# Masked maxima in one operation, scores issued ahead of the sums, and a quarter of the copies on VectorE, in a two-block network on one core

## The reference

```python
# sparse attention: 8 heads of 64, one key and value head, the selected keys of a row as mask
s = einsum(q, k_g) * 64 ** -0.5;  s = where(valid, s, -inf);  p = softmax(s);  o = p @ v_g
# latent attention: 8 heads, keys of 96, causal;  paired attention: 8 score maps in 4 pairs, causal
p = p[0] - lam * p[1]          # paired: mixed before the values
# memory attention: 4 heads of 128 against 256 memory tokens, no mask
```

```python
s = concat([einsum(q_row, k_win) + bias, einsum(q_row, k_c)]);  p = softmax(s)
o = p_loc @ v_win + p_ctx @ v_c
```

## Time and profile before

| | |
|---|---|
| median of 3 runs | 4144.8 us (4137.83 to 4156.16) |
| profiled execution, its own time | 4138.23 us |
| its span | 4136.4 us |
| mean granted TensorE clock | 0.973 of full |
| busy: TensorE, VectorE, ScalarE, GpSimd | 3854.7, 1670.0, 1430.4, 1414.1 us (93, 40, 35, 34%) |

### The profile page before, as it was taken

The page is one execution under the profiler, slowest core; times in us unless marked ns, Lnnn a source line. Parts: engine busy times, 40 slices in busy tenths (PEclk is TensorE's granted clock), DMA queues, the critical chain, the costliest instruction groups (busy, mean ns, idle before and its releaser), DMA issues. The chain is left out here.

```text
span 4136.4 us, 57230 instructions
## 1 busy us (share of the span) xinstructions
PE 3854.7 (93%) x23428; PEld 3229.0 (78%) x23428; DVE 1670.0 (40%) x3370; ACT 1430.4 (35%) x2322; POOL 1414.1 (34%) x525
## 2 busy tenths in 40 slices
PE   6998989999989899999989989999999888889999
PEld 5766878887876678788769967888888777867887
DVE  5845152322384524332261464311124676754111
ACT  3434242342234423333232364211122544433221
POOL 2211323343321132234322322223222567643342
PEclk8899999999999999999999999999999999999999
DMA  3221414434222142344412211112222111103332
GB/s 116 56 83 40 139 54 141 122 118 127 76 56 83 39 130 64 120 119 142 127 51 72 75 25 32 51 52 76 62 57 71 43 42 52 41 17 88 91 98 74
DMA packets 476080, 323.18 MB, mean 78 GB/s; under 512 B 31449, under 2 KB 472236, under 8 KB 475820
## 3 DMA queue, kind: packets, MB, share of 16 engines
q1 hardware_dynamic: 422112, 268.18, 22.5%
q10 hardware_dynamic: 53708, 51.33, 3.7%
HBM read 315.74 MB, written 2.16 MB: 77 GB/s over the span
## 5 line engine op out<-in xcount | busy, mean ns | idle before, releaser
L96 POOL TENSOR_TENSOR w_lo<-w_raw,w_hi 128x2048 fp32r<-128x2048 f32 (+6 forms) x329 | 1157.5, 3523 | 2417.8 <-ACT w_hi L228 2417.4
L228 ACT ACTIVATE w_hi<-w_raw 128x2048 fp32r<-128x2048 f32 (+3 forms) x278 | 471.9, 1698 | 1113.8 <-PE psum L264 1068.2
L262 PE MATMUL psum<-xF_hi,w_hi 128*128 128x512 f32 x1232 | 493.3, 400 | 15.7 <-ACT a_relud L1673 6.8
L264 PE MATMUL psum<-xF_hi,w_lo 128*128 128x512 f32 x1232 | 484.3, 393 | 0.0
L263 PE MATMUL psum<-xF_lo,w_hi 128*128 128x512 f32 x1232 | 480.7, 390 | 0.0
L262 PE MATMUL psum<-ffn_h_hi,w_hi 128*128 128x512 f32 (+1 forms) x1056 | 376.5, 357 | 2.2 <-issue 1.3
L264 PE MATMUL psum<-ffn_h_hi,w_lo 128*128 128x512 f32 (+1 forms) x1056 | 375.0, 355 | 0.0
L263 PE MATMUL psum<-ffn_h_lo,w_hi 128*128 128x512 f32 (+1 forms) x1056 | 373.7, 354 | 0.0
L262 PEld LDWEIGHTS psum<-xF_hi,w_hi 128*128 128x128 f32 x1232 | 232.6, 189 | 69.9 <-ACT a_relud L1673 8.4
L264 PEld LDWEIGHTS psum<-xF_hi,w_lo 128*128 128x128 f32 x1232 | 232.1, 188 | 53.8
L263 PEld LDWEIGHTS psum<-xF_lo,w_hi 128*128 128x128 f32 x1232 | 232.2, 189 | 48.7
(11 more groups left out here) (554 smaller groups left out, 8183.4 us busy)
## 6 DMA issues: line engine op xcount, KB each, us to landing
w_raw<-in_w_in_dram SPq DMA_DIRECT2D x56, 1024.0 KB, 5.2
ada_w<-in_ada_w_dram ACTq DMA_DIRECT2D x48, 1024.0 KB, 6.9
w_raw<-in_ffn_w_in_dram SPq DMA_DIRECT2D x88, 512.0 KB, 5.1
w_raw<-in_w_in_dram SPq DMA_DIRECT2D x78, 512.0 KB, 4.2
w_raw<-in_ffn_w_out_dram SPq DMA_DIRECT2D x32, 704.0 KB, 4.6
w_raw<-in_w_branch_dram SPq DMA_DIRECT2D x74, 256.0 KB, 4.6
w_raw<-in_hg_w_in_dram SPq DMA_DIRECT2D x32, 512.0 KB, 4.8
w_raw<-in_na_w_qkv_dram SPq DMA_DIRECT2D x12, 1024.0 KB, 5.1
```

The costliest lines, as they stand in the source:

```text
L96: return eng.tensor_tensor(pair.lo, src, pair.hi.bitcast(F32), ALU.subtract)
L228: act.activation(self.w(j).hi, self.raw_w(j), ACT.Copy).then_inc(*self.high_done.up(1))
L262: pe.matmul(out, left.hi, right.hi, start=first, stop=False)
L264: return pe.matmul(out, left.lo, right.hi, start=False, stop=last)
```

## The change

In the masked case the reduction's scale goes into `tensor_tensor_reduce`: it writes the negated scaled scores and reduces with a minimum, straight into `bias`; the exponential then has scale -1. Without a mask and with scale 1 (the context units of the neighbourhood stage), `tensor_reduce` negates. The `tensor_scalar` remains for the memory stage alone. Each unit now signals its own maximum. In `paired_attention` the same, and the tile `top` is gone.

TensorE's order in `attention` becomes scores(0), then for each s: turn(s-1), scores(s+1), sums(s-2). VectorE's: its copies of s-1, the maxima of s+1, the result of s-2, the inverse of s-1. ScalarE's: the copies of s-1, the exponentials of s+1, the raising of a part. In the neighbourhood stage units 3, 7, 11, ... 95 are in `dve_copies`.

```diff
                 C.enter(pe)
+                scores(0)
                 for s in range(NU // 2 + 2):
-                    if s < NU // 2:
-                        scores(s)
                     turn(s - 1)
+                    if s + 1 < NU // 2:
+                        scores(s + 1)
                     if features:
                         feature_sums(s - 2)
...
                     if mask is None:
-                        step(dve.tensor_reduce(column(top, u), scores_at(u)[:, 0:N], AX.X, ALU.max))
+                        if scale == 1.0:
+                            dve.tensor_reduce(column(bias, u), scores_at(u)[:, 0:N], AX.X, ALU.max, negate=True).then_inc(*max_found.up(1))
+                        else:
+                            step(dve.tensor_reduce(column(top, u), scores_at(u)[:, 0:N], AX.X, ALU.max))
+                            dve.tensor_scalar(column(bias, u), column(top, u), -scale, None, ALU.mult).then_inc(*max_found.up(1))
                     else:
...
-                        step(dve.tensor_tensor_reduce(dst, src, mask, 1.0, -3.0e38, ALU.add, ALU.max, column(top, u)))
-                    if not features:
-                        dve.tensor_scalar(column(bias, u), column(top, u), -scale, None, ALU.mult).then_inc(*max_found.up(1))
-                    elif u % 2:
-                        dve.tensor_scalar(columns(bias, u // 2), columns(top, u // 2), -scale, None, ALU.mult).then_inc(*max_found.up(2))
+                        dve.tensor_tensor_reduce(dst, src, mask, -scale, 3.0e38, ALU.add, ALU.min,
+                                                 column(bias, u)).then_inc(*max_found.up(1))
...
-                for s in range(NU // 2 + 2):
-                    for u in group(s):
+                for s in range(-1, NU // 2 + 2):
+                    for u in group(s - 1):
+                        if u in dve_copies:
+                            copy(u)
+                    for u in group(s + 1):
                         highest(u)
                     if features:
-                        for u in group(s - 1):
-                            if u in dve_copies:
-                                copy(u)
                         if s >= 2:
                             feature_result(s - 2)
...
-                for s in range(NU // 2 + 1):
-                    for u in group(s):
-                        N = width(u)
-                        act.wait_ge(*max_found.at(u + 1))
-                        if u >= 4:
-                            act.wait_ge(*turned.at(u - 3))
-                        src = scores_at(u)[:, 0:N] if units[u]["mask"] is None else probs[u % 4][:, 0:N]
-                        act.activation(probs[u % 4][:, 0:N], src, ACT.Exp, bias=column(bias, u), scale=scale,
-                                       accum_out=column(den, u)).then_inc(*exped.up(1))
+                for s in range(-1, NU // 2 + 1):
                     for u in group(s - 1):
...
+                    for u in group(s + 1):
+                        N = width(u)
+                        act.wait_ge(*max_found.at(u + 1))
+                        if u >= 4:
+                            act.wait_ge(*turned.at(u - 3))
+                        src, by = (scores_at(u)[:, 0:N], scale) if units[u]["mask"] is None else (probs[u % 4][:, 0:N], -1.0)
+                        act.activation(probs[u % 4][:, 0:N], src, ACT.Exp, bias=column(bias, u), scale=by,
+                                       accum_out=column(den, u)).then_inc(*exped.up(1))
...
-                    step(dve.tensor_tensor_reduce(probs[:, u % 6, 0:N], scores_at(u)[:, 0:N], units[u]["mask"], 1.0, -3.0e38,
-                                                  ALU.add, ALU.max, column(top, u)))
-                    dve.tensor_scalar(column(bias, u), column(top, u), -scale, None, ALU.mult).then_inc(*max_found.up(1))
+                    dve.tensor_tensor_reduce(probs[:, u % 6, 0:N], scores_at(u)[:, 0:N], units[u]["mask"], -scale, 3.0e38,
+                                             ALU.add, ALU.min, column(bias, u)).then_inc(*max_found.up(1))
...
-            dve_copies=())
+            dve_copies=range(3, NAH * TA, 4))
```

More of the change, by code:

```diff
@@ L952, in paired_attention @@
         probsT, probs = sb("probsT", [P, 2, 512]), sb("probs", [P, 6, 512])
-        top, bias, den, rec = (sb(n, [P, 8]) for n in ("top", "bias", "den", "rec"))
+        bias, den, rec = (sb(n, [P, 8]) for n in ("bias", "den", "rec"))
         share = sb("share", [P, 4])
@@ L1079, in _ @@
                             N = width(u)
-                            act.activation(probs[:, u % 6, 0:N], probs[:, u % 6, 0:N], ACT.Exp, bias=column(bias, u), scale=scale,
+                            act.activation(probs[:, u % 6, 0:N], probs[:, u % 6, 0:N], ACT.Exp, bias=column(bias, u), scale=-1.0,
                                            accum_out=column(den, u)).then_inc(*exped.up(1))
```

## The result

The changed kernel takes 4080.9 us (median of 4 runs, 4074.6 to 4096.8), against 4145.5 of the kernel before in 4 runs (4137.8 to 4156.2). The ratio is 0.985, 95% interval 0.981 to 0.988. The profiled execution took 4079.36 us, span 4077.6, where that of before took 4138.23 and 4136.4: 58.8 us less, against 37.5 in the sum of the prediction. On another chip, in 4 and 9 runs, they lay 58.0 apart (ratio 0.986, 0.984 to 0.987). What follows explains the 58.8.

What follows compares the result with a forecast made beforehand. TensorE, busy 93% of the 4136.4 us span, was taken as the bound, VectorE in the paired stages. Waits 29.3 + starts 3.4 + pairs 4.8 = 37.5 us, subtracted from the median 4144.8, gave 4107, range 4092 to 4128.

Steps and rivals of the forecast that it cites:

- Waits at the transposes: Neighbourhood, sparse, latent and memory stages: TensorE's waits for ScalarE's copies go, all but a tenth of 32.5 us: 29.3 us.
- rival B: Attention order: reordering does nothing, waits at L791 come back behind another releaser; 4135 us, chance 0.08.
- Starts: First exponential starts earlier: 1.0 us in the neighbourhood, 0.6 in each sparse and latent stage; 3.4 us, bounds 1 and 5.
- Pairs: Paired stages, bound by VectorE: 24 of 32 steps shed 0.20 us each, 4.8 us; bounds 2 and 9.
- Bounds: 60% of these 32.5 us (20) and all (33): Range for removing TensorE's listed waits in neighbourhood, sparse, latent and memory stages: at least 20 us, at most 33.
- rival C: TensorE's clock in the short stages: low stretches halve, 12 us more won, 4095; if they lengthen alike, 4119; chance 0.11.
- The median: Whole run: the profiled execution's 37.5 us saving subtracted unchanged from the median of runs, 4144.8, giving 4107.
- Copies: Neighbourhood: 24 of 96 copies move to VectorE, covered by TensorE's scores, costed at nothing; 14 us come back if uncovered.
- Minimum form: Masked maxima on VectorE: the combined operation with a minimum costs the same as the old one; no difference taken.
- rival D: VectorE's combined operations: the minimum form runs as something dearer; at double price 4168 us, chance 0.04.
- Rival A: Neighbourhood: bias tables become the bound, or VectorE's queue delays maxima; half the gain or more lost, 4121 to 4125, chance 0.13.
- signs that I had named for being wrong: Profile after: longer combined operations, new waits at L780 or L791, or short stages' granted clock moving by more than 0.05.

Runs made afterwards that it cites:

- the fillers: Changed kernel plus one or two unused constant matmuls while TensorE waits for the first exponentials of sparse, latent and neighbourhood stages: 4076.7 us (one run).
- The repeat: The changed kernel, unaltered, run once more on the same chip as a version with extra matmuls: 4085.0 us, ratio 0.9859 to the kernel before.

## Why the prediction was too cautious

**Waits at the transposes: 29.3 forecast, 32.5 measured, right.** All of the listed waits went, where I had left a tenth. No new one stands at L780 or L791. The neighbourhood's timeline, against the earlier trace rows (kernel after):

```profile
2404.09 1.14 PE L780 MATMUL psum<-na_k,na_a 64*128 64x256 f32 x8
...
2405.25 0.69 DVE L857 CUSTOM_DVE_ANT_1 na_b<-psum,na_T 128x512 f32<-128x512 f32 x1 [0.98 <-PE psum L780]
...
2405.96 1.09 PE L791 MATMUL psum<-consts,na_b 128*128 128x128 f32 x8
2405.99 0.72 ACT L925 ACTIVATE na_b<-na_b,consts 128x512 f32<-128x512 f32 x1 [0.41 <-DVE consts L857]
...
2407.09 0.69 DVE L885 COPY na_b<-psum 128x512 f32<-128x512 f32 x1
...
2409.29 1.09 PE L791 MATMUL psum<-consts,na_b 128*128 128x128 f32 x8
```

The scores end at 2405.23, the first exponential starts at 2405.99, 0.76 us later where it was 1.77; the transposes at 2405.96 are those of the step before, and come without idle time. My argument took both parts together, new order and shorter chain. The experiments show that either alone would have been enough for most of it, so the forecast was safer than I said, and rival B (the order does nothing) was wrong: alone it gives 15.0 us here. The stage came to 144.8 us where I had 148.

**Starts: 3.4 forecast, 3.4 measured.**

**Pairs: 4.8 forecast, 10.7 measured. This term of the sum was mis-sized.** The mechanism (VectorE bounds the stage; what counts is start to start) is right. The price of a step was wrong. The count of 24 fits, 24 x 0.44 = 10.6, but by luck, as no 24 steps shed this: from maximum to maximum the last ten steps of the first stage, and what follows them, are 0.42 us shorter each (3.03 became 2.60 at 512 keys), the first five together only 0.6, where VectorE now waits up to 0.54 us for TensorE's scores, and one step of the second stage, 3.03 to 1.81, is shorter by 1.2. I took 0.20 us and kept "up to 0.09 more if the wait for the read accumulator goes as well" as a bound; two waits went in a step, and each is 0.12. So even the bound of 9 was under the measured value. The trace of before had the numbers (VectorE, first paired stage):

```profile
612.55 0.68 DVE L1027 CUSTOM_DVE_ANT_0 probs_pairs<-psum,consts 128x512 f32<-128x512 f32 x1
613.16 0.09 DVE L1027 DVE_READ_ACCUMULATOR2_ANT top_pairs<- 128x1 f32 x1
```

The read starts 0.61 us after its maximum, the bias 0.12 after the read, the next maximum 0.12 after the bias: the whole 0.24 between the read and the next maximum was to be had, and 0.19 behind the second read (614.02 to 614.21). I counted only what stands behind the two biases, 0.12 and 0.08.

**"Bounds: 60% of these 32.5 us (20) and all (33)": the step that failed most, 11.2 us.** All that the wait view lists was taken as all that there was to gain, and the sum put the clock at nothing; only rival C, with a chance of 0.11, had it. Neither held: the idle time fell by what the list had, and 11.2 us more went from time in which TensorE is shown as busy. Rival C (12 us more, 4095) happened in part: 19.0 low microseconds went in the stages, in the direction that C had, but at 0.3 us each where C had 0.5. For the latent stages this is some 3 us, with the price from the fillers; for the sparse ones 4.6 fewer would make 1.4 at that price, which no run isolates. The Trainium skill (TensorE: Matmul & The Clock Gate, Part 1) has the throttled state as the default from which activity releases the clock; the fillers agree, 6.9 low microseconds to 0.0 in each latent stage, the one matmul in the sparse stages changed nothing. The rest of the 11.2, about 7 us, went from inside the steps, where the profile shows TensorE as busy. In one latent stage the comparison at full clock shows 1.8 us of it; for the others it is what is left over, and its cause is open.

**The median.** 4144.8 - 58.8 is 4086; the measured 4080.9 is another 5 lower because the two profiled runs stood 7 and 2 us under their medians, and I had assumed the same distance. The repeat's 4085.0 shows how far this moves.

**Copies: nothing forecast, nothing measured. Minimum form: same price forecast, same measured.** VectorE's combined operations in the sparse stages (kernel after; least, median, most in ns):

```profile
L857 DVE CUSTOM_DVE_ANT_0 probs_dsa<-psum,a_sel x64: 285/488/692, 190.3 to 1251.5; 128x128 f32<-128x128 f32 x16, 128x256 f32<-128x256 f32 x16, 128x384 f32<-128x384 f32 x16, 128x512 f32<-128x512 f32 x16
```

Against 291/492/693 in the earlier trace rows: rival D falls. Rival A, that the bias tables become the bound, also falls, but the margin is thin. GpSimd's completions (kernel after, timeline; the bracket is idle time before, and what ended it):

```profile
2341.19 4.15 POOL L2440 TENSOR_TENSOR na_T<-na_whole,consts 128x256 f32<-128x256 f32 x6 [15.11 <-DMA na_whole<-bias_rows]
2358.29 4.16 POOL L2440 TENSOR_TENSOR na_T<-na_whole,consts 128x256 f32<-128x256 f32 x6 [12.94 <-DMA na_whole<-bias_rows]
...
2443.26 4.16 POOL L2440 TENSOR_TENSOR na_T<-na_whole,consts 128x256 f32<-128x256 f32 x6 [10.65 <-DMA na_whole<-bias_rows]
```

All seven wait for transfers alone, 16.6 to 17.8 us apart, 17.0 in the mean, and a pair of heads now takes 144.8/8 = 18.1. No wait of VectorE for a table is listed. By these numbers I estimate that a further gain of some 8 us in this stage would meet them; that was not tried.

The sum for rival D was loose: it takes 8 us as what is left of the gain, where my own terms leave 2.4 + 0.8 + 1.2 + 4.8 = 9.2. None of the signs that I had named for being wrong showed: no longer operation, no new wait, and no stage's clock moved by more than 0.05 (the second latent stage moved by just that). They looked for losses; none looked for a gain beyond the list.

**What stays open.** Which of the fewer low microseconds in the sparse and paired stages belong to the change: the same kernel gave 58.3 and 66.3 in two profiles. What the 7 us inside the steps are, of which 1.8 are measured at full clock. And what lengthens the stretches outside the stages by up to 8 us from profile to profile.

## What to carry to other kernels

Price an operation that leaves the queue of a bounding engine by the distance from start to start with and without it, its wait on itself included: here the wait was worth as much as the instruction. When a loop of dependent steps is a little too long for the work that covers it, one removed link is enough; two are not worth twice as much, so test each alone before keeping both. Don't take a list of waits as the upper bound of what a change can win: here 11.2 us more came out of time shown as busy. And look at the granted clock behind a pause at the start of a short stage: in the latent stages here a wait of 2 us had 6.8 us of low clock behind it. Compare stages and whole runs both, and repeat a profile before explaining a few microseconds.

## What the runs showed of the hardware that I had not expected

- A maximum of 512 columns with an accumulator output, 0.68 us long in the trace, lets the next such operation start 0.60 us after its own start, together with its accumulator read; a wait on that output makes it 0.72.
- In the latent stages the low time was 6.8 to 7.0 us in all 8 stages of the 4 profiles with the new order and no filler, and 10.7 to 17.6 in those of the old order and no filler, with TensorE shown busy in most of it. A low microsecond cost 0.26 to 0.35 us there. Two matmuls of 512 columns in the first wait made it 0.0 in five of six stages.
- The same reduction with another pair of operations (add and maximum, add and minimum) has the same duration, 0.29 us for 128 and 0.69 for 512 columns.
- The same stretch of some 2600 matmuls between two stages, with the same mean clock of 0.98, took 392.6 us in one profile and 399.1 and 399.3 in two others.
